# A fused two-block transformer kernel on one core: the last weighted selection of the second mixture a step earlier, and the output made and stored in four pieces

## What is computed

```python
def hier_moe(h, w_rg, b_rg, w_re, b_re, w1e, w3e, w2e):
    ...
    cw = jnp.sum(jax.nn.one_hot(flat_idx, N_EXPERTS_2, dtype=f32) * wts[..., None], axis=1)
    ...
    for e in range(N_EXPERTS_2):
        he = jax.nn.silu(t @ w1e[e]) * (t @ w3e[e])
        out = out + cw[:, e:e + 1] * (he @ w2e[e])
...
        x = x + gt2[:, None, :] * hier_moe(h2, ...)
    shf, scf = jnp.split(c_act @ w_ada_f + b_ada_f, 2, axis=-1)
    return modulate(rmsnorm_2(x, g_final), shf, scf)   # norm * g_final * (1 + scf) + shf
```

## Time and profile before

| | |
|---|---|
| median of 3 runs | 2201.53 us (2201.14, 2201.53, 2204.37) |
| the profiled execution | 2203.47 us, of which the span is 2202.2 us |
| PE busy | 2045.3 us (93%) |
| DVE, ACT, POOL busy | 732.3, 294.1, 156.8 us (33%, 13%, 7%) |
| mean granted clock of PE | 0.975 of full |
| data moved | 648.59 MB, mean 295 GB/s |
| chain that ended last | PE 76%, DMA 16%, DVE 3%, ACT 2% |

### The profile page before, as it was taken

The page is one execution under the profiler, slowest core; times in us unless marked ns, Lnnn a source line. Parts: engine busy times, 40 slices in busy tenths (PEclk is TensorE's granted clock), DMA queues, the critical chain, the costliest instruction groups (busy, mean ns, idle before and its releaser), DMA issues.

```text
span 2202.2 us, 22437 instructions
## 1 busy us (share of the span) xinstructions
PE 2045.3 (93%) x9478; PEld 1075.9 (49%) x9478; DVE 732.3 (33%) x1230; ACT 294.1 (13%) x644; POOL 156.8 (7%) x207
## 2 busy tenths in 40 slices
PE   3989999999999999999999999999889999989997
PEld 1654467856453333333333333333368898553332
DVE  2177758435221111111101111111159544332213
ACT  1111130122021011111101111110024121110000
POOL 3122511010000000000000000000020100000100
PEclk7999999999999999999999999999989999989999
DMA  7598720131738999999999999999932212739995
GB/s 278 225 410 340 295 77 23 45 128 57 267 141 375 396 428 427 427 428 428 428 428 427 428 427 427 427 428 427 378 113 87 106 39 92 310 141 421 420 422 209
DMA packets 91992, 648.59 MB, mean 295 GB/s; under 512 B 10032, under 2 KB 15384, under 8 KB 47568
## 3 DMA queue, kind: packets, MB, share of 16 engines
q1 hardware_dynamic: 87216, 640.41, 70.8%
q0 software_dynamic: 4672, 6.68, 1.0%
HBM read 645.94 MB, written 1.11 MB: 294 GB/s over the span
## 4 chain that ended last, share of the span: by engine, by line
PE 76%; DMA 16%; DVE 3%; ACT 2%; issue 1%; POOL 0%; SPq 0%; POOLq 0%; DVEq 0%; ACTq 0%
PE ps L218 34%; PE ps L1661 14%; DMA sb<-in_w_down 8%; PE ps L1688 7%; DMA sb<-in_w_gate_up 6%; PE ps L2563 5%; PE ps L1404 5%; PE ps L2587 3%; PE ps L1650 2%; PE ps L223 2%; PE ps L604 2%; DMA sb<-in_w_in 1%; PE ps L621 1%; PE ps L2035 1%; DVE sb L973 1%
## 5 line engine op out<-in xcount | busy, mean ns | idle before, releaser
L218 PE MATMUL ps<-sb 128*128 128x128 f32 (+4 forms) x3782 | 827.1, 381 | 35.9 <-DMA sb<-in_w_in 10.2
L218 PEld LDWEIGHTS ps<-sb 128*128 128x128 f32 (+1 forms) x3782 | 578.9, 193 | 271.5 <-issue 213.8
L1661 PE MATMUL ps<-sb 128*64 128x512 f32 x2048 | 449.9, 596 | 1.3 <-DMA sb<-in_w_gate_up 0.6
L1661 PEld LDWEIGHTS ps<-sb 128*64 128x64 f32 x2048 | 143.8, 137 | 305.2 <-issue 291.7
L1688 PE MATMUL ps<-sb 128*64 128x512 f32 x1024 | 233.8, 612 | 49.6 <-DMA sb<-in_w_down 28.3
L1778 DVE TENSOR_SCALAR sb<-ps 128x512 f32<-128x512 f32 x32 | 33.6, 1049 | 491.6 <-PE ps L1661 491.6
L1688 PEld LDWEIGHTS ps<-sb 128*64 128x64 f32 x1024 | 87.5, 140 | 185.1 <-issue 185.1
L1415 DVE TENSOR_TENSOR sb<-ps,sb 128x512 f32<-128x512 f32 x64 | 44.3, 692 | 383.9 <-PE ps L1688 294.7
L1744 ACT COPY sb<-ps 128x512 f32<-128x512 f32 x32 | 18.8, 586 | 787.5 <-PE ps L223 787.5
L2563 PE MATMUL ps<-sb 128*64 128x512 f32 x512 | 114.4, 600 | 4.3 <-POOL sb L2660 3.7
L1404 PE MATMUL ps<-sb 128*128 128x512 f32 x256 | 115.3, 593 | 1.7 <-DVE sb L1415 1.7
(11 more groups left out here) (338 smaller groups left out, 1144.6 us busy)
## 6 DMA issues: line engine op xcount, KB each, us to landing
sb<-in_w_gate_up SPq DMA_DIRECT2D x128, 2048.0 KB, 23.8
sb<-in_w_down SPq DMA_DIRECT2D x64, 2048.0 KB, 26.3
sb<-in_w_in SPq DMA_DIRECT2D x24, 2048.0 KB, 8.3
sb<-in_w1e SPq DMA_DIRECT2D x32, 1024.0 KB, 16.0
sb<-in_w3e SPq DMA_DIRECT2D x32, 1024.0 KB, 18.1
sb<-in_w2e SPq DMA_DIRECT2D x32, 1024.0 KB, 19.9
sb<-in_w_ada SPq DMA_DIRECT2D x24, 1024.0 KB, 8.9
sb<-in_w_mod SPq DMA_DIRECT2D x16, 1024.0 KB, 12.2
```

Source lines behind the costliest of these rows:

```text
L218: last = te.matmul(o, l, r, start=i == 0, stop=i == len(pairs) - 1)
L1661: last = te.matmul(ps[64 * h:64 * h + 64, 512 * c:512 * c + 512], xg[k][:, t, 64 * m:64 * m + 64], w[:, at:at + 512], start=False, stop=t ...
```

## The change

- In `vector_moe2`, the two memsets stand in front of `vector_logits`.
- In `compact_places`, the three shifted copies of the places are written behind the first selection's release, with a `settle()` behind them.
- `choose_weights(1, 15)` is called in step 15, between the activation and the scalings, and no longer in step 16.
- `combine` counts `outh` for each 512 columns of each half, and `vector_add_out` adds in four pieces of 512 columns (both mixtures); `x4` is counted by the second piece of each half.
- `vector_last` first writes `x * gf` into `xs_last` (the storage of `xn2`, as plain 128 x 2 x 1024), a half at a time, then makes the output as `xs_last * rstd + shf` in four pieces of 512 columns. It waits for the squares as well, since it writes over `x`.
- `sync_last` stores four pieces of 256 KB, in rows of 2 KB.

```diff
@@ compact_places
                 for i in range(2):
                     ve.tensor_scalar(sel4[:, b, i, :], slot, at[:, 2 * i:2 * i + 1], None, ALU.is_equal).then_inc(dv.up(), 1)
-                if b == 0:
-                    for k in range(1, 4):
-                        ve.tensor_scalar(place[:, k, :], dest, -128.0 * k, None, ADD).then_inc(dv.up(), 1)
                 settle()
...
                 last.then_inc(s["sel"], 1)
+                if b == 0:
+                    for k in range(1, 4):
+                        ve.tensor_scalar(place[:, k, :], dest, -128.0 * k, None, ADD).then_inc(dv.up(), 1)
+                    settle()
@@ combine
-                if last:
-                    done.then_inc(s["outh"], 1)
+                    if last:
+                        done.then_inc(s["outh"], 1)
@@ vector_add_out
             for i in range(2):
-                ve.wait_ge(s["outh"], 2 * m + i + 1)
-                ve.tensor_tensor(x[:, i, :], OUT[:, i, :], x[:, i, :], ADD).then_inc(s["x4"], 1)
+                for n in range(2):
+                    cols = slice(512 * n, 512 * n + 512)
+                    ve.wait_ge(s["outh"], 4 * m + 2 * i + n + 1)
+                    ve.tensor_tensor(x[:, i, cols], OUT[:, i, cols], x[:, i, cols], ADD) \
+                        .then_inc(s["x4"] if n else dv.up(), 1)
@@ vector_moe2
-            vector_logits(1, lg2, 36)
             ve.memset(g8, -3e38).then_inc(dv.up(), 1)
             ve.memset(lem, -3e38).then_inc(dv.up(), 1)
+            vector_logits(1, lg2, 36)
             settle()
...
-                if p:
+                if 0 < p < 16:
                     choose_weights(1, p - 1)
...
                     ve.tensor_tensor(he[k], th2[k], b, MUL).then_inc(s["he"], 1)
+                if p == 15:
+                    choose_weights(1, 15)
@@ the last norm
+        xs_last = xn2.rearrange("p i t q -> p i (t q)")
...
         def vector_last():
             for i in range(2):
+                ve.wait_ge(s["x4"], 3 + i)
+                ve.tensor_tensor(xs_last[:, i, :], x[:, i, :], gf, MUL).then_inc(dv.up(), 1)
+            settle()
+            for i in range(2):
+                ve.wait_ge(s["sq"], 19 + i)
                 ve.wait_ge(s["rstd"], 14 + i)
-                ve.scalar_tensor_tensor(x[:, i, :], x[:, i, :], stat[:, 8 + i:9 + i], gf, MUL, MUL).then_inc(dv.up(), 1)
-                settle()
-                ve.tensor_tensor(x[:, i, :], x[:, i, :], shf, ADD).then_inc(s["res"], 1)
+                for n in range(2):
+                    cols = slice(512 * n, 512 * n + 512)
+                    ve.scalar_tensor_tensor(x[:, i, cols], xs_last[:, i, cols], stat[:, 8 + i:9 + i], shf[:, cols], MUL, ADD) \
+                        .then_inc(s["res"], 1)
@@ sync_last
-                sp.wait_ge(s["res"], i + 1)
-                sp.dma_start(ov[i], x[:, i, :]).then_inc(s["out"], 16)
-            sp.wait_ge(s["out"], 32)
+                for n in range(2):
+                    cols = slice(512 * n, 512 * n + 512)
+                    sp.wait_ge(s["res"], 2 * i + n + 1)
+                    sp.dma_start(ov[i][:, cols], x[:, i, cols]).then_inc(s["out"], 16)
+            sp.wait_ge(s["out"], 64)
```

## The result

The changed kernel takes 2195.4 us in the median of 16 runs (2190.65 to 2198.18), the kernel before 2201.57 (2195.3 to 2204.37, 16 runs). The ratio is 0.9974, 95% interval 0.9965 to 0.9983, so 5.7 us less, between 3.7 and 7.7. The prediction said 2198.4, 3.1 us less, with a range from 2196.6 to 2200.9. The direction is right, the size is not.

The account below looks back on a forecast made before the run. PE and the weight stream are full through the second mixture, so only its head, last pairs and tail can pay: 0.39 + 1.2 + 0.87 + 0.63 = 3.1 us, from 2201.5 to 2198.4, range 2196.6 to 2200.9.

Parts of the forecast that it names:

- The last selection: Last pairs of the second mixture: selecting pair 15's weights one step earlier saves 1.2 us, bounds 1.1 and 1.35.
- (b): Head of the second mixture: shifting the places behind the first release starts the second pair and PE 0.22 us earlier.
- (a): Head of the second mixture: two memsets moved before the logits save 0.17 us, between 0 and 0.19.
- (h): End of the first mixture: its sum in pieces gains 0, as DVE goes on at 1597.63 either way; bounds 0 and 0.53.
- What differs between the runs: Whole kernel: the change leaves run differences untouched, so the forecast starts from the median of three timed runs, 2201.53.
- (c to e): Tail: sum in four pieces, DVE's 5.2 us in a row from 2193.45; gain 0.87 us, bounds 0.3 and 1.35.
- (f): Tail: POOL waits out DVE's two products, norm ready about 2196.3, hidden with 1.0 us in hand; no cost to DVE.
- Rival 2: Tail: ports held for a whole instruction, POOL delays DVE 0.5 to 0.75 us; sum 2.4, 2199.1; chance 0.12.
- (g): Last store: 256 KB instead of 512 KB halves the data time, 0.63 us less; bounds 0 and 0.9.
- The third rival: Jump hidden (0.5), first mixture 0.5, small store 0.2, combine 0.15 more; sum 4.4 or more, 2197.1 and below; chance 0.17.

Follow-up runs that it names:

- p_pieces: The kernel before with only the sums of both mixtures added, and released by PE, in four pieces; median 2198.58 us, ratio 0.9992.
- p_last: The kernel before with only the last norm and the four stores changed; median 2199.26 us, ratio 0.9983.
- p_head: The kernel before with only the two memsets before the logits and the three shifted places behind the first release; median 2199.71 us, ratio 0.9991.
- the experiment: The changed kernel with two stores of 512 KB in place of four of 256 KB; median 2197.12 us of 8 runs.

## Why the prediction was wrong

It gave 3.1 us, and its range ended at 2196.6; measured are 5.7 (5.5 over all runs). The steps, read from the traces, come to 3.8, so 0.7 of the miss is in the sum and the rest outside it. Step by step:

- **The last selection**, 1.2: right, 1.24, and the wait that takes its place is the one named, the combine behind the scaling, 0.28 us after the turn.
- **The places** (b), 0.22: right, 0.22. **The memsets** (a), 0.17: wrong, they brought nothing. The copy did start 0.24 us sooner, but the row that showed it at 0.40 us was that of a held instruction: POOL's clearing ran beside it. I priced the gap in front of it and not its end.
- **The first mixture's sum** (h), 0, is the step that failed. I took the 16 KB packet at 1597.2 for what DVE's next instruction waited for, so that the earlier norm could not help. After the change DVE goes on at 1596.71, 0.12 behind POOL's power as before, while the packet of that place moves in 1597.0:1597.2. It came too late to be the cause. The step gives 0.54 (0.53 in p_pieces), the upper bound named.
- **What differs between the runs** is the larger miss. The sum's paragraph says that the change does not touch it, and gives no reason. The profiles say that it does, through the same step (h): with PE's wait 0.5 us shorter, the long stretch at 1.2 GHz was not seen again, some 1.5 us in the mean. How much of the excess this makes, and how much is chance, stays open. The page of before had it: a slice with the clock at less than full behind the first mixture, and runs 3.2 us apart. No rival priced it.
- **The tail** (c to e), 0.87: DVE ended 1.18 sooner. The 5.2 us in a row were 5.13. From the last piece's start to the next instruction it was 0.92 us where I had 1.16; the bounds 0.3 to 1.35 hold it. The 1.16 came from the distance between packet and instruction behind the first mixture, and there DVE had waited for POOL, as (h) shows. Here the packet, which moves in 2188.2:2188.4, is right in front of DVE's start at 2188.42; that DVE waited for it is likely but not shown.

```profile
q8 instruction: 1, 0.02, 35.2%
```

- **POOL against DVE** (f): right. POOL's power took 1.40 us beside the products and ended 0.4 behind them; DVE waited for nobody. Rival 2 had DVE 0.5 to 0.75 us later. But DVE's first piece began at 2190.81, while POOL's power ran to 2191.19, and the four pieces took 2.74 us, 0.69 each. POOL's scaling ran its plain 0.19 us across the boundary of two products that took 2.36 together, and 2.37 in p_last. The Trainium skill's rule that whichever starts first holds the shared ports for its whole instruction (SBUF — State Buffer, SBUF: two separate sides) is thus not what these rows show for DVE behind POOL. Its other part, that the second one waits, fits POOL's power, which ended 0.41 us behind the products, and DVE's copy, which ended 0.03 us behind POOL's clearing in the kernel before, the changed one and p_head. The order does not fit the copy: in the last two it starts first, 0.06 and 0.05 us before the clearing.
- **The store** (g), 0.63: right, 0.63, by the experiment 0.62.
- The third rival, more than forecast, is what happened, but not for its reasons: it had the jump hidden and the combine's wait free, and neither is so.

## What to carry to other kernels

Where the matmul engine waits some us between two stages, its clock is part of the price: read the granted clock behind each wait, in several profiles, and ask what half a microsecond more or less does to it. Products of constants in four such waits took 4 to 5 us out of this kernel, more than any one part of the change. When a kernel runs faster than its steps explain, run it again before looking for a cause: here the 21 later runs had a mean 2.1 us above the first 16. And before a gap is priced, look at the instruction behind it: if it ends with another engine's, the gap is not on the path.

## What the runs showed of the hardware

- Without fillers the half-speed stretch behind one and the same wait was 6.8 us long in nine profiles and 13.7 in five. In the short ones PE's work began 2.7 to 4.1 us after the clock fell, in the long ones 4.4 to 4.6.
- A DVE copy of 8 columns took 0.63 us beside a POOL memset of 0.54 us, which reads nothing, and 0.17 without it; with the memset it ended 0.03 us behind it, though it had started 0.06 us before it.
- A store of 256 KB in rows of 2 KB lands 2.0 us after its issue, one of 512 KB in rows of 4 KB 2.6. Four of them issued 0.7 us apart still took 2.0 each in the median.
- Behind a jump over unused code, DVE's next instruction came 0.92 us after its last one before the jump had started, right after a 16 KB packet of the instruction queue; that it waited for the packet is not shown. Behind an instruction of 0.69 us this leaves 0.23 us idle; behind one of 1.22 us (p_last) nothing.
